# An expert layer on Trainium2: 128 slots in three split products, or 96 slots as three groups of 32 with unsplit weights in four column tiles

## The chip, the cores and the metric

One core of one Trainium2 chip. The metric is the device time of a run in microseconds; before the change the median of 3 runs is 1737.04 (1737.0 to 1737.24). Differences under 0.2% of that are not told from none.

## The reference

Two layers of a decoder trunk over 256 tokens of width 1024, all in float32: a mixer sub-layer with three token mixers, a cross-attention into a memory of 256 rows, and a channel sub-layer, which is a dense SwiGLU in layer 0 and eight experts in layer 1. The change touches only the experts:

```
def swiglu(h, w_gate, w_up, w_down):
    return (silu(h @ w_gate) * (h @ w_up)) @ w_down       # 1024 -> 2816 -> 1024

def moe_swiglu(h, w_router, w_gate, w_up, w_down):
    top_val, top_idx = lax.top_k(h @ w_router, 2)          # of 8 experts
    top_w = softmax(top_val)
    for e in range(8):
        out = out + comb[..., e:e+1] * swiglu(h, w_gate[e], w_up[e], w_down[e])
```

Each expert's three matrices are 34.6 MB, all eight 276.8 MB. For the given inputs the reference's own routing sends 74, 67, 63, 59, 76, 59, 64 and 50 of the 512 choices to the eight experts.

## The kernel before, in words

Each engine runs its own instruction list; semaphores order them. The list of the expert stage (layer 1) is built by `one_pass(p)` on every engine, which goes over the experts n = 0 to 7. A pass gives each expert 128 slots for tokens. A second pass stands in the program behind a branch (`moe_passes`, L588), and runs when an expert has more than 128 tokens.

The rows. The router's logits and counts give each token its slot. Expert 0's rows are gathered by a product with a 0/1 matrix (`gather`, L3328). Meanwhile GpSimd writes all rows of h, ordered by expert, to HBM with four indirect DMAs (L978), and later loads an expert's 128 rows as `h_e` (L983); TensorE transposes them (`turn_rows`, L3343) into `fx_e`, k on the partitions, slots on the free axis. The results of experts 0 to 6 are stored to `y_rows_d` in HBM (L986, L988), fetched per token by indirect DMA (L994) and added on VectorE. Expert 7's result is scattered by a product (`scatter`, L3350), added to x by VectorE (`add_scattered`, L2478 to L2484), and the last norm and the store of the output follow.

The products. float32 operands are split in a high and a low part of type fp32r, and a product is three matmuls (`split_product`, L3226): hi·hi, hi·lo, lo·hi. The stationary operand is a 128 x 128 block (128 of K, 128 slots), the moving one 128 x 512 of the weights. An expert is worked in chunks of 512 of its 2816 hidden columns, five full and one of 256: gate and up products (`input_group`, L3389), tanh on ScalarE (L1603), gating and multiplication by up on VectorE (`gated` L2514, `times_up` L2524), four transposes of the result (`flip`, L3370, counted under L3375), their split (L1595, L2508), and the down product (`output_groups`, L3400) into two PSUM banks. A chunk's flip stands inside the next chunk's gate product, and its down product after that chunk's up product.

The weights. SyncE's queue loads them in pieces of 128 partitions x 4096 floats (2 MB) into a ring of four buffers (L806 down, L815 gate and up, L823 the short chunk). A gate or up piece has runs of 512 columns (2 KB) in HBM, a down piece runs of 1024 (4 KB). A piece goes through `piece_hi` on ScalarE (L1089, copy to fp32r) and `piece_lo` on VectorE (L1696, subtraction) in two halves of 2048 columns, into four split buffers. SyncE may reuse a ring buffer when VectorE has split it, ScalarE a split buffer when TensorE has used it. The first four pieces are issued while the cross-attention of layer 1 still runs.

Elsewhere in the kernel unsplit float32 products occur. One form stands in the trace as two matmul records and two weight loads. Two of them are used below: full-array products of 128 x 256 (L2755), and the output of the state-space mixer, four column tiles of 32 each with its own moving operand:

```
for c in range(2):
    for i, r_ in enumerate(S5_ROWS):                       # r_ = 32 partitions of the bank
        last = mm(y_bank[r_, HS:SEQ], cT[:, c, q, r_], h(i, c), start=c == 0, stop=c == 1)
```

Of the kernel before, what the change touches and what calls it, by code (L numbers as in the profile page):

```python
# [7 lines left out]
def hybrid_trunk(nc: bass.Bass, x_d, mem_d, positions_d, norm_mix_d, w_in_d, a_re_d, a_im_d, log_dt_d,  # L8
# [40 lines left out]
    NPIECE, PIECE = 4, 4096  # L49
    NBUF, HGRP = 4, 2048  # L50
    assert D_FF == NFULL * FW + FC
# [61 lines left out]
    with ctx:  # L113
# [55 lines left out]
        gain_out = ring[:, NPIECE * PIECE:NPIECE * PIECE + D]  # L169
# [104 lines left out]
        def flat(v):  # L274
# [39 lines left out]
        rf.take(2 * KD * P + 2 * FC // P * SEQ)  # L314
        r_log = rf.take(NT, NE)
# [13 lines left out]
        gather_m = rf.take(NT, P)  # L329
        weight_m = rf.take(NT, P)  # L330
        scatter_m = rf.take(NT * P)
        y_e = rf.take(D)
# [4 lines left out]
        row_buf = [ring[:, NPIECE * PIECE + D:NPIECE * PIECE + 2 * D], h_e]  # L337
# [7 lines left out]
        y_rows_d = nc.dram_tensor("y_rows_d", ((NE - 1) * P + 1, D), F32, kind="Internal").ap()  # L345
# [13 lines left out]
        fx_e = [over("fx_e0", [P, 2, KD, P], phase_at + 4 * op_at),  # L359
                over("fx_e1", [P, 2, KD, P], qk_at + 4 * (6 * NT * W + 4 * D))]  # L360
        f_actT_e = over("f_actT_e", [P, 2, FW // P, P], phase_at + 4 * (op_at + 2 * KD * P))
        mf_th, mf_a, mf_act = (phase[:, i * FW:(i + 1) * FW] for i in range(3))
        split_e = [over("split_e0", [P, 2, HGRP], qk_at), over("split_e1", [P, 2, HGRP], qk_at + 8 * HGRP),
                   over("split_e2", [P, 2, HGRP], phase_at + 4 * end_at), over("split_e3", [P, 2, HGRP], hT_at)]
        assert 4 * HGRP <= 6 * NT * W + 2 * D and end_at + 2 * HGRP <= PH
        HI, LO = 0, 1

# [71 lines left out]
        B = [ctx.enter_context(nc.psum_tensor(f"bank{i}", [P, 512], F32)) for i in range(8)]  # L439
# [6 lines left out]
        piece_full = [slot_full[0], slot_full[1], sem("piece_full2"), slot_full[2]]  # L446
        split_hi, split_lo, split_used = sem("split_hi"), sem("split_lo"), sem("split_used")
        fx_hi, fx_ready, actT_hi = sem("fx_hi"), sem("fx_ready"), sem("actT_hi")
        ab_in, bc_nat_in = sem("ab_in"), sem("bc_nat_in")
        consts = sem("consts")  # L450
# [137 lines left out]
        def moe_passes(eng, one_pass, final=None):  # L588
            more = one_pass(0)
            if final is not None:  # L590
                with eng.If(more < 1):
                    final(0)
            with eng.If(more > 0):
                one_pass(1)
                if final is not None:
                    final(1)

        def last_piece(e, i):
            return (i % 2, i // 2) if e == NE - 1 else (i // 2, i % 2)
# [3 lines left out]


        def piece_base(l, s):
            return 0 if s == 2 else slot_after_unit(l, NUNIT - NSLOT + min(s, 2))

        group_at, piece_at, piece_end, piece_sum = {}, {}, [], []

        def count_piece(kind, n, c):  # L610
            half = c == NFULL
            s = len(piece_end) % NPIECE
            piece_at[kind, n, c] = len(piece_end)
            for i in range(1 if half and kind == "d" else 2):
                group_at[kind, n, c, i] = len(group_at)
            piece_end.append(len(group_at))
            piece_sum.append((piece_sum[-NPIECE] if len(piece_sum) >= NPIECE else 0)
                             + (32 if half and kind == "g" else 16))

        for p_ in range(2):  # L620
            for n_ in range(p_ * NE, (p_ + 1) * NE):
                for c_ in range(NFULL + 1):
                    count_piece("g", n_, c_)
                    if c_ < NFULL:
                        count_piece("u", n_, c_)
                    if c_ > 0:
                        count_piece("d", n_, c_ - 1)
                    elif n_ > p_ * NE:
                        count_piece("d", n_ - 1, NFULL)
            count_piece("d", (p_ + 1) * NE - 1, NFULL)  # L630

        def chunk_at(n, c):
            return n * (NFULL + 1) + c

        def chunk_before(n, c):
            return (n, c - 1) if c > 0 else (n - 1, NFULL)
# [9 lines left out]
        def scattered(n):  # L646
            return n >= NE - 1

# [3 lines left out]
        def closes(n, c):  # L652
            return n % NE == NE - 1 and c == NFULL

        def y_copies(n):
            return n + 1 if n < NE - 1 else NE - 1 + 2 * (n - (NE - 1) + 1)

        def act_buf(n, c):
            return fx_e[(n + 1) % 2] if closes(n, c) else f_actT_e
# [3 lines left out]

        def down_groups(c):
            return 2 if c < NFULL else 1

        def bank_turn(n, c, up):
            return n * (2 * NFULL + 1) + 2 * c + up

        def gate_bank(n, c):  # L670
            return bank_turn(n, c, 0) % 3

        def up_bank(n, c):
            return bank_turn(n, c, 1 if c < NFULL else 0) % 3
# [17 lines left out]
        def _(sp):  # L692
# [94 lines left out]
            def expert_pieces(l):  # L787
# [21 lines left out]
                def one_pass(p):  # L809
                    for e in range(NE):  # L810
                        n = p * NE + e
                        for c in range(NFULL):
# [4 lines left out]
                            if c > 0:  # L817
                                load_down(e, n, c - 1)
                            elif e > 0:
                                load_down(e - 1, n - 1, NFULL)  # L820
# [2667 lines left out]
```

## Time and profile before

| what | value |
|---|---|
| median of 3 runs | 1737.04 us |
| span of the profiled execution | 1733.9 us, 3.1 us under the median of the runs |
| PE / PEld busy | 1691.8 us (98%) / 1377.0 us (79%) |
| DVE / ACT / POOL busy | 1391.5 us (80%) / 1058.7 us (61%) / 158.5 us (9%) |
| HBM read | 422.93 MB, 250 GB/s over the span |
| granted TensorE clock, mean | 0.997 |

The execution's own time is known as its span, from the first to the last instruction. PE is TensorE's matmuls, PEld its weight loads, DVE VectorE, ACT ScalarE, POOL GpSimd, SP SyncE. Matmuls are pipelined and their ends are modelled, so that their recorded durations overlap: the pace is read from the distance between starts, not from a duration. A group's first row says how to read its view.

### The profile page before, as it was taken

The numbers are of one execution on the slowest core, as the hardware profiler recorded it, in microseconds if no ns is written. First come the engines' busy times: TensorE is split into PE (matmuls) and PEld (weight loads), VectorE is DVE, ScalarE is ACT, GpSimd is POOL, SyncE is SP. The second block draws the span as 40 slices with busy tenths as digits, with TensorE's granted clock in tenths as the row PEclk, the third lists the DMA queues.
The fourth block names the chain that finished last, engine by engine and source line by source line (L and its number), as shares of the span: only waits on it lengthen the run. The fifth ranks groups of instructions, "written<-read, shape, count | busy, mean of one in ns | idle before, by whom it ended". The sixth has DMA issues, their size and how long they took to land. (4 is left out here: it accounts for less than half of the span.)

```text
span 1733.9 us, 23684 instructions
## 1 busy us (share of the span) xinstructions
PE 1691.8 (98%) x9485; PEld 1377.0 (79%) x9485; DVE 1391.5 (80%) x1770; ACT 1058.7 (61%) x1228; POOL 158.5 (9%) x218
## 2 busy tenths in 40 slices
PE   8999999999999999999999999999999999999997
PEld 5778877788888888887778788888888888888885
DVE  5799677765555599967775899989998989899997
ACT  4335665555444533566556677777777777687765
POOL 7430002000000343000200100000000000000010
PEclk9999999999999999999999999999999999999999
DMA  9444543256551644444135699999999999999994
GB/s 269 146 146 164 177 146 135 98 194 217 195 192 50 212 147 146 162 178 146 50 110 206 243 391 380 396 368 395 373 395 370 393 388 378 390 376 390 356 397 167
DMA packets 220196, 434.93 MB, mean 251 GB/s; under 512 B 19180, under 2 KB 63864, under 8 KB 220088
## 3 DMA queue, kind: packets, MB, share of 16 engines
q1 hardware_dynamic: 213704, 419.45, 67.1%
q0 software_dynamic: 3520, 11.76, 1.8%
q10 hardware_dynamic: 2864, 2.23, 0.4%
q8 instruction: 73, 1.20, 0.3%
q14 instruction: 35, 0.29, 0.0%
HBM read 422.93 MB, written 10.49 MB: 250 GB/s over the span
## 5 line engine op out<-in xcount | busy, mean ns | idle before, releaser
L1696 DVE TENSOR_TENSOR split_e<-ring,split_e 128x2048 fp32r<-128x2048 f32 x264 | 598.4, 2287 | 40.2 <-ACT split_e L1089 39.9
L1089 ACT ACTIVATE split_e<-ring 128x2048 fp32r<-128x2048 f32 x264 | 503.3, 1919 | 149.5 <-PE bank L3230 130.9
L3228 PE MATMUL bank<-split_e,fx_e 128*128 128x512 f32 x708 | 280.3, 396 | 1.2 <-DVE split_e L1696 0.6
L3230 PE MATMUL bank<-split_e,fx_e 128*128 128x512 f32 x708 | 276.3, 390 | 0.0
L3229 PE MATMUL bank<-split_e,fx_e 128*128 128x512 f32 x708 | 275.8, 390 | 0.0
L3228 PEld LDWEIGHTS bank<-split_e,fx_e 128*128 128x128 f32 x708 | 133.0, 188 | 28.2 <-issue 0.8
L3230 PEld LDWEIGHTS bank<-split_e,fx_e 128*128 128x128 f32 x708 | 132.9, 188 | 28.3
L3229 PEld LDWEIGHTS bank<-split_e,fx_e 128*128 128x128 f32 x708 | 133.1, 188 | 26.3
L3228 PE MATMUL bank<-split_e,f_actT_e 128*128 128x512 f32 x348 | 136.1, 391 | 0.0
L3230 PE MATMUL bank<-split_e,f_actT_e 128*128 128x512 f32 x348 | 135.5, 389 | 0.0
L3229 PE MATMUL bank<-split_e,f_actT_e 128*128 128x512 f32 x348 | 135.4, 389 | 0.0
L1078 ACT ACTIVATE ring_r<-ring 128x1024 fp32r<-128x1024 f32 x71 | 73.9, 1057 | 53.5 <-PE bank L2781 47.1
L1690 DVE TENSOR_TENSOR ring_r<-ring,ring_r 128x1024 fp32r<-128x1024 f32 x71 | 84.7, 1219 | 22.6 <-ACT ring_r L1078 22.5
L2755 PE MATMUL bank<-hT,ring 128*128 128x256 f32 x384 | 85.0, 381 | 0.0
L2755 PEld LDWEIGHTS bank<-hT,ring 128*128 128x128 f32 x384 | 72.3, 190 | 10.6 <-issue 0.4
L3230 PEld LDWEIGHTS bank<-split_e,f_actT_e 128*128 128x128 f32 x348 | 65.3, 188 | 13.6
L3229 PEld LDWEIGHTS bank<-split_e,f_actT_e 128*128 128x128 f32 x348 | 65.4, 188 | 13.3
L3228 PEld LDWEIGHTS bank<-split_e,f_actT_e 128*128 128x128 f32 x348 | 65.3, 188 | 13.3
L3228 PE MATMUL bank<-split_mix,fx 128*128 128x512 f32 x168 | 66.4, 396 | 0.0
L3230 PE MATMUL bank<-split_mix,fx 128*128 128x512 f32 x168 | 65.5, 390 | 0.0
L3229 PE MATMUL bank<-split_mix,fx 128*128 128x512 f32 x168 | 65.4, 389 | 0.0
L1683 DVE TENSOR_TENSOR split_mix<-ring,split_mix 128x1024 fp32r<-128x1024 f32 x44 | 51.9, 1219 | 2.3 <-ACT split_mix L1057 1.6
(647 smaller groups left out, 3277.9 us busy)
## 6 DMA issues: line engine op xcount, KB each, us to landing
ring<-in_moe_w_gate SPq DMA_DIRECT2D x40, 2048.0 KB, 13.5
ring<-in_moe_w_up SPq DMA_DIRECT2D x40, 2048.0 KB, 13.4
ring<-in_moe_w_down SPq DMA_DIRECT2D x40, 2048.0 KB, 13.4
ring<-in_w_in SPq DMA_DIRECT2D x27, 2048.0 KB, 7.9
ring<-in_ffn_w_gate SPq DMA_DIRECT2D x11, 1024.0 KB, 5.4
ring<-in_ffn_w_up SPq DMA_DIRECT2D x11, 1024.0 KB, 8.0
ring<-in_ffn_w_down SPq DMA_DIRECT2D x11, 1024.0 KB, 8.7
ring<-in_ssm_w_glu SPq DMA_DIRECT2D x8, 1024.0 KB, 6.3
```

The source lines that it names most:

```text
L1078: nc.scalar.activation(unit_hi(l, m), unit_raw(j, i), ACT.Copy).then_inc(split_hi, 1)
L1089: nc.scalar.activation(split_e[j % NBUF][:, HI, :], ring[:, s * PIECE + i * HGRP:s * PIECE + (i + 1) * HGRP], ACT.Copy).then_inc(split_hi, 1)
L1683: V.tensor_tensor(split[buf][:, LO, :], raw_group(s, i), split[buf][:, HI, :].bitcast(F32), ALU.subtract).then_inc(split_lo, 1)
L1690: V.tensor_tensor(unit_lo(j, i), unit_raw(j, i), unit_hi(l, m).bitcast(F32), ALU.subtract).then_inc(split_lo, 1)
L1696: V.tensor_tensor(split_e[j % NBUF][:, LO, :], ring[:, s * PIECE + i * HGRP:s * PIECE + (i + 1) * HGRP], split_e[j % NBUF][:, HI, :].bitca ...
L2755: last = mm(B[t][:, (m % 2) * SEQ:(m % 2 + 1) * SEQ], w[:, k, m * P:(m + 1) * P], hT[:, k, :], start=k == 0, stop=k == KD - 1)
L3228: mm(bank, a[HI], w[HI], start=first, stop=False)
L3229: mm(bank, a[HI], w[LO], start=False, stop=False)
L3230: return mm(bank, a[LO], w[HI], start=False, stop=last_one)
```

## The change

The split of the expert weights goes, with `piece_hi`, `piece_lo`, `tail_hi`, `tail_lo`, `gathered_lo` and the fp32r buffers. Slots per expert become 96, as three groups of 32, with up to three passes behind the branch. Weights are used as they arrive, in unsplit float32 products of 128 x 32 stationary and 256 (in the last chunk 192) moving columns, four at a time in four column tiles that write to four quadrants of 32 PSUM partitions:

```
+        CAP, TG, GS = 96, 3, 32
+        CW = (1024, 1024, 768)
-        NPIECE, PIECE = 4, 4096
-        NBUF, HGRP = 4, 2048
+        NPIECE, PIECE, RING_PIECES = 7, 4096, 4

+                    def gate_or_up(kind, n, c):
...
+                        for i in range(2):
...
+                            cols = arrived_piece(kind, n, c, i)[:, 0:4 * CW[c]].rearrange("p (k f) -> p k f", f=CW[c])
+                            for k in range(4):
+                                kk = 4 * i + k
+                                for g in range(TG):
+                                    for j, r_ in enumerate(QUADS):
+                                        last = mm(out[r_, g, 0:w], fx_e[n % 2][:, kk, g * GS:(g + 1) * GS],
+                                                  cols[:, k, j * w:(j + 1) * w], start=..., stop=...)
+                            last.then_inc(split_used, 1)

+                    def down(n, c):
...
+                        for i in range(2):
+                            w = arrived_piece("d", n, c, i).rearrange("p (k n) -> p k n", n=D)
+                            for k in range(4 * i, min(4 * i + 4, last_k + 1)):
+                                for g in range(TG):
+                                    for j, r_ in enumerate(QUADS):
+                                        last = mm(y_out_bank[r_, g, :], acts(v, c, g, k), w[:, k % 4, j * CQ:(j + 1) * CQ],
+                                                  start=..., stop=...)

+                            for c in range(NC):
+                                gate_or_up("g", n, c)
+                                gate_or_up("u", n, c)
+                                if c == 1:
+                                    if closes(n):
+                                        turn_weights(n)
+                                    else:
+                                        turn_rows(n + 1)
+                                if chunk_before(n, c) is not None:
+                                    down(*chunk_before(n, c))
+                                flip(n, c)
+                            if closes(n):
+                                down(n, NC - 1)
+                                scatter(n)
```

A chunk is now 1024, 1024 or 768 hidden columns. Its gate and up results lie side by side in one of two sets of three banks (group by group, column quarter j in partition quadrant j), so tanh, gating and multiplication each run once over 128 x 3 x 256. The flip makes two transposes per group; in the last chunk one transpose and two products with a part of the identity, since a quarter is 192 wide:

```
+                    def flip(n, c):
...
+                        for g in range(TG):
+                            last = tr(to[:, g, 0:P], mf_act[:, g, 0:P], ident[:, :])
+                            if c < NC - 1:
+                                last = tr(to[:, g, P:2 * P], mf_act[:, g, P:2 * P], ident[:, :])
+                            else:
+                                for b in range(2):
+                                    last = mm(to[b * 64:(b + 1) * 64, g, P:192].rearrange(...), mf_act[:, g, P:192],
+                                              ident[:, :].rearrange(...)[:, b], start=True, stop=True)
```

A weight piece is still 128 x 4096 floats (3072 in the last chunk's gate and up), now four k tiles of 1024 columns, so its runs in HBM are 4 KB (3 KB). There are seven buffers, four in the ring and three over the space of q, k and the gates. A buffer is free when TensorE has used it:

```
+                free_after = [multiplied(l, U_OUT + 1), multiplied(l, U_WQ), multiplied(l, U_WQ), multiplied(l, U_WQ),
+                              (xs_o, XH * (l + 1)), multiplied(l, U_WO), (rows_in, 16 * ROWS_LAID)]
...
+                    if j >= NPIECE:
+                        sp.wait_ge(split_used, USED + j - NPIECE + 1)
+                    else:
+                        sp.wait_ge(*free_after[j])
```

ScalarE copies the gathered or turned rows and the flipped activations out of PSUM as they are. Expert results are stored to HBM in four DMAs instead of one. The last expert's result is scattered by products of K = 32 in four row tiles, and added to x in two additions of 1024 columns instead of four of 512.

## Rows read from the trace of the kernel before

**Rows 1.** Window sums: stretch, length, busy us (records) of each engine, PEclk, DMA share, GB/s.
```profile
960.00:974.00 14.00, 11.15 (x75) 10.81 (x73) 10.95 (x41) 6.77 (x13) 0.00 (x0) 0.76 0.79 299
974.00:1721.50 747.50, 746.64 (x3402) 617.86 (x3403) 682.29 (x437) 553.83 (x388) 21.99 (x22) 1.00 1.00 372
```

**Rows 2.** Records of one line (row turns): duration min/median/max, first and last start.
```profile
L3347 PE MATMUL bank<-ident,phase x56: 270/272/273, 1046.9 to 1607.6; 128*128 128x128 f32 x56
```

**Rows 3.** Waits from 1100 to 1600: us in total, times, longest.
```profile
ACT split_e L1089 <- PE bank L3230: 101.4, 142, 1.1
...
ACT split_e L1089 <- DMA ring<-in_moe_w_up: 0.9, 1, 0.9
```

**Rows 4.** Timeline of TensorE: start us, us, instruction; x4 is four merged.
```profile
1130.20 0.39 PE L3228 MATMUL bank<-split_e,fx_e 128*128 128x512 f32 x1
...
1130.88 0.39 PE L3228 MATMUL bank<-split_e,fx_e 128*128 128x512 f32 x1
...
1239.62 0.40 PE L3230 MATMUL bank<-split_e,f_actT_e 128*128 128x512 f32 x1
1239.85 0.60 PE L3375 MATMUL bank<-ident,phase 128*128 128x128 f32 x4
...
1240.53 0.39 PE L3229 MATMUL bank<-split_e,fx_e 128*128 128x512 f32 x1
```

**Rows 5.** Page, part 5: instruction groups, busy us, mean ns, idle before.
```profile
L1696 DVE TENSOR_TENSOR split_e<-ring,split_e 128x2048 fp32r<-128x2048 f32 x264 | 598.4, 2287 | 40.2 <-ACT split_e L1089 39.9
...
L3228 PE MATMUL bank<-split_e,fx_e 128*128 128x512 f32 x708 | 280.3, 396 | 1.2 <-DVE split_e L1696 0.6
...
L3228 PE MATMUL bank<-split_e,f_actT_e 128*128 128x512 f32 x348 | 136.1, 391 | 0.0
```

**Rows 6.** DMA: stretches of 4 KB packets and of 2 KB packets; issues with us to landing.
```profile
DMA packets 402, 1.65 MB, mean 412 GB/s; under 512 B 0, under 2 KB 0, under 8 KB 402
...
DMA packets 743, 1.54 MB, mean 384 GB/s; under 512 B 0, under 2 KB 0, under 8 KB 742
...
ring<-in_moe_w_gate SPq DMA_DIRECT2D x40, 2048.0 KB, 13.5
```

**Rows 7.** Timeline at the stage's start.
```profile
974.02 0.50 PE L3228 MATMUL bank<-split_e,fx_e 128*128 128x512 f32 x1 [0.36 <-DVE fx_e L2500]
...
993.04 0.60 POOL L983 DMA_DIRECT2D phase<-h_rows_d  x1 [7.70 <-DMA h_rows_d<-gates,row_at]
```

**Rows 8.** Timeline of TensorE around a tiled stretch; 128\*32 is rows and columns in use.
```profile
654.75 0.38 PE L2755 MATMUL bank<-hT,ring 128*128 128x256 f32 x1
655.06 0.42 PE L2826 MATMUL bank<-uT,phase 128*32 128x128 f32 x8
655.30 0.62 PE L2829 MATMUL bank<-phase 128*32 128x127 f32 x16
655.74 0.62 PE L2832 MATMUL bank<-phase 128*32 128x128 f32 x16
...
656.28 0.70 PE L2755 MATMUL bank<-hT,ring 128*128 128x256 f32 x2
...
656.82 4.26 PE L2755 MATMUL bank<-hT,ring 128*128 128x256 f32 x19
```

**Rows 9.** Instruction groups of ScalarE and VectorE, 1100 to 1600.
```profile
L1603 ACT ACTIVATE phase<-bank 128x512 f32<-128x512 f32 x27 | 15.7, 581 | 3.6 <-PE bank L3230 3.6
...
L2514 DVE SCALAR_TENSOR_TENSOR phase<-phase,bank 128x512 f32<-128x512 f32 x27 | 18.3, 680 | 0.0
```

**Rows 10.** Timeline at the end.
```profile
1721.53 3.94 PE L3358 MATMUL bank<-phase 128*128 128x512 f32 x8
...
1725.51 0.69 DVE L2484 TENSOR_TENSOR x<-x,bank 128x512 f32<-128x512 f32 x1 [0.27 <-PE bank L3358]
```

**Rows 11.** Weight loads of a tiled line: ns min/median/max.
```profile
L2829 PEld LDWEIGHTS bank<-phase x128: 110/110/110, 91.7 to 721.3; 128*32 128x32 f32 x128
```

**Rows 12.** Window sums: the 16 us with the most TensorE records.
```profile
276.97:292.97 16.00, 15.48 (x330) 13.30 (x332) 12.29 (x21) 5.81 (x11) 6.78 (x10) 1.00 0.44 142
```

More of the change, by code:

```diff
@@ L328, in hybrid_trunk @@
         over_i = sb("over_i", [P, 1], I32)
[L329 to L332, printed above, removed]
+        gather_m = rf.take(NT, CAP)
+        weight_m = rf.take(NT, TG, 4 * GS)
+        y_e = rf.take(TG, CQ)
+        re = Region(phase, rf_end)
+        fx_e = [re.take(KD, CAP) for _ in range(2)]
+        actT_e = [re.take(TG * CQ) for _ in range(2)]
+        scatter_m = re.take(NT, TG, P)
         xg = memT[:, :, :].rearrange("p k n -> p (k n)").rearrange("p (t n) -> p t n", t=NT)
@@ L608, in hybrid_trunk @@
[L608 to L630, printed above, removed]
         def chunk_at(n, c):
-            return n * (NFULL + 1) + c
+            return n * NC + c
@@ new lines, in count_piece @@
+        def count_piece(kind, n, c, i):
+            piece_at[kind, n, c, i] = len(piece_sum)
+            piece_sum.append((piece_sum[-NPIECE] if len(piece_sum) >= NPIECE else PIECE_BASE[len(piece_sum)])
+                             + (32 if kind == "d" and c == NC - 1 and i == 1 else 16))
+        for n_ in range(NALL):
+            for c_ in range(NC):
+                for kind_, nc_ in (("g", (n_, c_)), ("u", (n_, c_)), ("d", chunk_before(n_, c_))):
+                    if nc_ is not None:
+                        count_piece(kind_, *nc_, 0)
+                        count_piece(kind_, *nc_, 1)
+            if closes(n_):
+                count_piece("d", n_, NC - 1, 0)
+                count_piece("d", n_, NC - 1, 1)
@@ L3400, in output_groups, with scatter @@
-                    def output_groups(n, c, between=None):
-                        pe.wait_ge(actT_ready, base + chunk_at(n, c) + 1)
+                    def scatter(n):
+                        pe.wait_ge(sm_ready, scatter_turn(n) + 1)
+                        for t in range(NT):
+                            for g in range(TG):
+                                if g != 1:
+                                    pe.wait_ge(ye_ready, y_copies(n) - 1 + g // 2)
+                                for j, r_ in enumerate(QUADS):
+                                    last = mm(B[4 * t + j][:, 0:CQ], scatter_m[r_, t, g, :], y_e[r_, g, :],
+                                              start=g == 0, stop=g == TG - 1)
+                            last.then_inc(sc_ps, 1)
@@ new lines, in down @@
+                        last_k = 5 if ends else 7
+                        if ends and closes(n):
+                            w = [arrived_piece("d", n, c, i).rearrange("p (k n) -> p k n", n=D) for i in range(2)]
+                            for g in range(TG):
+                                for k in range(6):
+                                    for j, r_ in enumerate(QUADS):
+                                        last = mm(y_out_bank[r_, g, :], acts(v, c, g, k), w[k // 4][:, k % 4, j * CQ:(j + 1) * CQ],
+                                                  start=False, stop=k == last_k and g > 0)
+                                if g > 0:
+                                    last.then_inc(*((y_half, 1) if g == 1 else (split_used, 2)))
+                            return
```

571 lines of the change are left out of this document (225 added, 346 removed).

## The prediction

> **What bounds the kernel now.** I read the window sums first, to find the stretch that the change touches: the expert stage runs from 974.0 to 1721.5 us of the span and TensorE is busy through all of it [rows 1]. The last transpose of the last row turn starts 560.7 us after the first of the first, six experts earlier [rows 2]; less the seven transposes between (0.8), that is 93.3 us an expert, and 8 × 93.3 = 746.4 accounts for the stage. Next the waits: ScalarE waits for TensorE to hand back a split buffer (101.4 us in 500), for a weight DMA once (0.9 us) [rows 3]. So the others wait for TensorE. Last the pace inside: three products from 1130.20 to 1130.88 are 227 ns each, and from 1239.62 to 1240.53 two such steps, which else take 0.45 us, take 0.91 with four transposes between them, 0.11 each [rows 4]. An expert has 132 (k tile × 512 columns) blocks of three products: 396 × 0.227 = 89.9, and 22 + 8 transposes × 0.112 = 3.4; sum 93.3, the measured period, without any stall. The lines give the same counts: (708 + 348) / 8 = 132 [rows 5].
>
> DMA is the close second. The stage reads 372 GB/s, and a 2 MB piece lands 13.5 us after its issue although TensorE eats one every 24 × 0.227 = 5.4 us: two or three are always in flight [rows 1, 6]. With 4 KB runs alone the queue moves 412 GB/s, with 2 KB runs 384, at the same busy share of 102 to 103% [rows 6].
>
> **The change part by part.** *Splits out.* 264 VectorE subtractions and as many ScalarE copies go [rows 5]. They run beside TensorE and TensorE is not short of them: worth nothing on the path, except 0.5 us at the start, where TensorE waited until 974.02 for VectorE's half of the gathered rows [rows 7] and will now wait for the gather and ScalarE's copy only.
>
> *The products.* Now one unsplit fp32 product for K = 128, 32 slots, 256 columns, in each of four column tiles; three groups of 32 slots. I call four such products a round. The kernel before does the same in a small way: 128\*32 tiles with four different moving operands, 127 or 128 columns. A matmul of this kind stands in the trace as two passes. 16 passes take from 655.30 to 655.74, so four tiles' passes take 0.11 us together, what one tile's 128 columns would take alone: the tiles overlap fully [rows 8]. 256 columns are shown on the full array: (4.26 − 0.38) / 18 = 0.216 us a pass [rows 8]. I take 2 × 0.216 = 0.432 us for a round of 256 columns, and for the third chunk's 192 columns halfway between the two rows, 2 × 0.163 = 0.326. From below the cost is bounded by the 0.11 for 128 columns, doubled (0.44 a round, the same); from above by no overlap at all (4 × 0.432), which the 0.11 speaks against.
> An expert has for gate and up 2 × 8 k × 3 groups × 2 chunks = 96 rounds, 41.5 us, and 48 narrow ones, 15.6; for down 22 k × 3 = 66, 28.5. Sum 85.6 us against 89.9. The column count streamed is the same (96 slots unsplit cost what 128 slots in three products cost); the gain is that a pass costs 216 ns where the split product costs 227.
>
> *Transposes.* Flips 6 + 6 + 3, the row turn 8: 23 × 0.109 = 2.5 us; six 64-column products in the third flip, some 0.1 each (nearest the 0.11 rows), 0.5 in all.
>
> *Changes of tiling.* New: the array goes from 32-column tiles to full width and back four times an expert (three flips, the row turn), and inside the third flip five times between 128 and 64. From full to tiled, the first tiled pass starts 0.31 us after the last full one instead of 0.22, and the first round is 0.02 longer: 0.12. Back, 0.21: the last 16 passes start at 655.74 and would be through at 656.18, the full one starts at 656.28 and its successor 0.32 later, not 0.22 [rows 8]. 4 × 0.33 + 5 × 0.17 = 2.2 us. Bounds: zero, and twice that.
> An expert on TensorE: 85.6 + 2.5 + 0.5 + 2.2 = 90.8 us; eight, 726.4.
>
> *New exposed waits.* (a) The first chunk of the first expert has no down product between its up product and its flip. Tanh, gating and multiplication over 768 columns, one and a half times the 512-column rows (0.58, 0.68, 0.68) [rows 9], with 0.4 for hand-overs: 3.3 us once. Everywhere else 7.8 or 10.4 us of down product cover it. Behind the flip stand all of TensorE's later products. (b) The last flip is followed at once by its own down product: copy 0.87 + hand-overs 0.5 = 1.4 us.
> Stage: 726.4 + 3.3 + 1.4 = 731.1, against 747.5: −16.4.
>
> *DMA and its queue.* Seven buffers instead of four; SyncE issues in order, and piece 6 waits until the four indirect row stores have landed. They had at 993.04 [rows 7]; VectorE's part ahead of them loses a 2.3 us subtraction and the low halves, so about 989. The rest of the queue stands behind it. TensorE eats a piece in 12 rounds = 5.2 us from 973.5 on, with the 3.3 us stall after four, so it needs piece 6 at 1007 and piece 7 at 1012; issued at 989, they land by 996 and 1002. Hidden, with 10 us to spare; if the stores were 10 us later, each further us would be lost. Per expert 34.6 MB: 28.3 in 4 KB runs at 412 GB/s, 6.3 in 3 KB runs at the middle of the two rows, 398; 0.9 MB of rows and some fetch of the doubled instruction stream, 3.2 us: 87.7 us, under the 90.8. Storing y rows as four DMAs instead of one, and waits for them, have an expert's time to hide in.
>
> *Ends.* The scatter is 6 rounds (2.6 us) instead of 8 passes of 3.94, but its adds are 1024 wide and the last y copy is exposed; before, the last add starts 4.0 us after the scatter [rows 10]. +0.3.
>
> Sum: −0.5 − 16.4 + 0.3 = −16.6. The profiled span 1733.9 becomes 1717.3; the median of the runs lies 3.1 above that span, so **1720.5 us**.
>
> **A rule that speaks against it.** Row: in the tiled stretch every pass has its own weight load of 110 ns and the passes of a tile still follow each other every 0.11 us, so the loads are hidden [rows 8, 11]. The Trainium skill (TensorE: Matmul & The Clock Gate, "What overlaps and what doesn't") says that a weight load overlaps running matmuls only where its row group differs, which column tiles never offer; the trace disagrees for 128 columns. Its "Measured speedup" table gives three column tiles 2.38×, not 3×; an estimate by that share, 85.6 / 0.79, would be 108 us an expert and some 1899 us in all.
>
> **The rivals.**
> 1. *TensorE's instruction issue* (slower). A round is 16 instructions, 27 ns each at 256 columns and 20.4 at 192, for 15.6 us on end. For: the densest 16 us of the trace hold 330 + 332, that is 24.2 ns each [rows 12]. Against: TensorE also waits for others there, and the 32 matmuls and loads of 0.44 us came at 14 ns each [rows 8]. Were 24.2 a limit, each narrow round would take 387 instead of 326 ns: 48 × 0.061 × 8 = +23.4, **1744**. Above 23.1 ns it eats the whole gain (16.6 / 8 / 48 = 43 ns a round); at 30 ns the wide rounds suffer too, 1840.
> 2. *Weight loads not hidden at 256 columns* (slower): a round is 2 × (0.216 + 0.110), 0.546 narrow; 131.7 us an expert, +369: **2090**. This is the mechanism of the Trainium skill's rule above.
> 3. *DMA becomes the bound.* For: 87.7 against 90.8 is close, and after the change nothing shares the blame. All at 384 GB/s, the 272.6 MB that come after 989 are down at 1699, plus the last down product 7.8 and 2 for landing: 3 to 4 us late, **1724**; at the whole stage's 372, 1747. Against: 4 KB runs go faster [rows 6].
> 4. *Changes of tiling cost nothing*: TensorE needs 88.6, DMA 87.7: −17.6, **1703**.
> 5. *More than one pass*, if an expert had over 96 tokens: each pass repeats the stage. The reference's routing gives 74, 67, 63, 59, 76, 59, 64, 50, so no.
> The clock is a surcharge: it is granted at 0.76 on the mean in the router's gaps from 960 to 974 [rows 1]. If the 3.3 us stall brings it from 2.4 to 1.2 GHz for as long as there (0.24 × 14 × 2 = 7 us), 3.4 us are lost.
>
> **How the numbers follow.** Forecast 0.58, its own range 1711 to 1730. Rival 1: 0.15; 2: 0.04; 3: 0.12; 4: 0.10; 5: 0.01. Reaching to rivals 3, 4 and the near end of 1 leaves under 0.2 out: 1702 to 1743. A difference under 0.2% (3.5 us) can't be told from none. Faster: 0.58 + 0.10 + 0.09 = 0.77; same 0.07 (parts of 1 and 3); slower 0.16.
>
> **What would show it.** The distance between the first records of two row turns: 90.8 us (rival 4: 88.6; 1: 93.7 or more). Passes of a tile 216 ns apart, rounds in the third chunk 326; 387 there with 432 elsewhere is rival 1. A gap of 0.33 around each flip. One TensorE gap of 3.3 us ended by VectorE near 994, one of 1.4 before the last down product. TensorE waiting for DMA at most a few us in all; tens of us are rival 3. The forecast is wrong if TensorE's period is above 93 or below 89.

## The result, and the profile after

The changed kernel takes **1752.09 us** (median of 4 runs, 1750.18 to 1758.12); the kernel before took 1737.02 us on the same chip. The ratio is 1.0091, 95% interval 1.0074 to 1.0109: the change makes the kernel 0.9% slower. The forecast was 1720.5 us, range 1702 to 1743.

The page of the changed kernel (the first row of the span, the engines, and of part 3 the queue that brings instructions; columns as before):

```profile
span 1751.2 us, 43424 instructions
...
PE 1682.7 (96%) x19841; PEld 1251.6 (71%) x19841; DVE 752.3 (43%) x1396; ACT 548.2 (31%) x909; POOL 164.4 (9%) x239
...
q8 instruction: 153, 2.51, 0.6%
```

VectorE and ScalarE lost nearly half of their busy time, as the diff says, and it bought nothing. The window sum of the expert stage, to be set beside [rows 1]:

```profile
975.00:1743.00 768.00, 740.15 (x13746) 492.60 (x13738) 53.89 (x64) 54.03 (x80) 27.00 (x43) 0.99 0.98 360
```

The DMA engines are about as busy as before (0.98 against 1.00), but 372 GB/s have become 360. The records of the row turns, which answer to [rows 2]:

```profile
L3259 PE MATMUL banks<-ident,phase x56: 272/273/331, 1022.7 to 1582.9; 128*128 128x128 f32 x56
```

From the first transpose to the last (560.2 us) less the seven between (0.8) and over six experts, an expert takes 93.2 us. Forecast was 90.8, before it was 93.3. The six single distances rise: 91.2, 92.2, 93.3, 93.3, 93.7, 95.8. From the first transpose of the last row turn to the scatter's first product go another 153.8 us.

What TensorE waited for from 975 to 1740 (us in total, times, longest), to be set beside [rows 3]:

```profile
PE banks L3362 <- DMA ring<-in_moe_w_down: 6.1, 3, 4.3
PE banks L3312 <- issue: 5.9, 11, 1.1
PE banks L3312 <- DMA ring<-in_moe_w_up: 3.3, 4, 2.1
PE banks L3322 <- DVE phase L2478: 2.9, 1, 2.9
PE banks L3312 <- DMA past_ring<-in_moe_w_up: 2.3, 2, 2.1
PE banks L3362 <- issue: 1.4, 3, 0.6
PE banks L3352 <- ACT phase L1600: 0.7, 1, 0.7
PE banks L3312 <- DMA past_ring<-in_moe_w_gate: 0.7, 2, 0.5
```

Two things are new: waits for weights (12.4 us here), and "issue", gaps with no releaser in the profile (7.3 us). The 2.9 is the first flip, as forecast, and the 0.7 for ScalarE is the last one. Last, window sums within one expert:

```profile
1100.00:1153.00 53.00, 52.12 (x1028) 35.48 (x1024) 3.42 (x4) 3.15 (x5) 0.56 (x1) 1.00 1.02 400
1154.00:1164.00 10.00, 10.00 (x174) 6.11 (x175) 0.00 (x0) 0.65 (x1) 0.00 (x0) 1.00 1.03 229
1165.00:1240.00 75.00, 74.59 (x1438) 51.42 (x1434) 5.33 (x6) 5.56 (x8) 2.75 (x5) 1.00 1.03 404
```

For ten microseconds DMA moves 229 GB/s while the 16 engines show as fully busy. In the records of the packets, one of 4 KB takes about 300 ns there and 164 ns elsewhere. Such a stretch comes once an expert, in the place in the queue where the last chunk's down pieces stand. That is where the search began.

The end of the chain of waits (start us, us, what) shows what the shortage costs late, when the seven buffers' lead is used up:

```profile
1690.20 27.69 DMA ring<-in_moe_w_down
...
1717.93 7.74 PE banks L3362 x96
...
1728.00 7.98 PE banks L3352 x144
1735.98 1.56 PE banks L3281 x24
```

The first line is a down piece on its way for 27.69 us. TensorE waits 4.3 us for it and then runs at a granted clock of 0.51 (1.2 GHz) from 1715.9 to 1722.8: the x96 are 12 rounds, which took 7.7 us and not the 5.2 they need at 2.4 GHz.

### The profile page after: what moved, and what is told of

Read it like the earlier page. It is cut to its first block, busy times and chain, and to the rows that moved or that the text cites. A ratio compares the mean times of both kernels' runs of the same rounds, so it can differ in the third digit from the quotient of the medians.

```text
span 1751.2 us, 43424 instructions
## 1 busy us (share of the span) xinstructions
PE 1682.7 (96%) x19841; PEld 1251.6 (71%) x19841; DVE 752.3 (43%) x1396; ACT 548.2 (31%) x909; POOL 164.4 (9%) x239
## 4 chain that ended last, share of the span: by engine, by line
PE 81%; DMA 7%; DVE 6%; ACT 4%; issue 1%; POOL 1%; SPq 0%; DVEq 0%; ACTq 0%
PE banks L3312 23%; PE banks L3362 11%; DMA ring<-in_moe_w_up 5%; PE banks L2668 5%; PE banks L3141 3%; PE banks L3143 3%; PE banks L3142 3%; PE banks L2693 3%; PE banks L2697 3%; PE banks L2694 3%; PE banks L2601 3%; PE banks L2605 3%; PE banks L2602 3%; DMA ring<-in_moe_w_down 2%; PE banks L2876 1%; PE banks L2577 1%
## 5 line engine op out<-in xcount | busy, mean ns | idle before, releaser
L3312 PE MATMUL banks<-ring,phase 128*32 128x256 f32 (+1 forms) x5184 | 269.4, 363 | 6.9 <-DMA ring<-in_moe_w_up 3.3
L3312 PEld LDWEIGHTS banks<-ring,phase 128*32 128x32 f32 x5184 | 172.8, 110 | 95.8 <-issue 8.5
L3312 PE MATMUL banks<-past_ring,phase 128*32 128x256 f32 (+1 forms) x4032 | 210.9, 363 | 5.5 <-issue 2.5
L3312 PEld LDWEIGHTS banks<-past_ring,phase 128*32 128x32 f32 x4032 | 135.0, 111 | 74.0 <-issue 8.4
L3362 PE MATMUL banks<-ring,phase 128*32 128x256 f32 x2496 | 144.8, 384 | 6.7 <-DMA ring<-in_moe_w_down 6.1
L3362 PEld LDWEIGHTS banks<-ring,phase 128*32 128x32 f32 x2496 | 96.8, 111 | 49.3 <-issue 7.6
L3362 PE MATMUL banks<-past_ring,phase 128*32 128x256 f32 x1584 | 91.2, 379 | 0.8 <-issue 0.8
L2668 PE MATMUL banks<-hT,ring 128*128 128x256 f32 x384 | 85.0, 381 | 0.0
L2668 PEld LDWEIGHTS banks<-hT,ring 128*128 128x128 f32 x384 | 72.3, 190 | 10.6 <-issue 0.4
L3362 PEld LDWEIGHTS banks<-past_ring,phase 128*32 128x32 f32 x1584 | 59.8, 110 | 27.8 <-issue 2.5
L3141 PE MATMUL banks<-split_mix,fx 128*128 128x512 f32 x168 | 66.5, 396 | 0.0
L3143 PE MATMUL banks<-split_mix,fx 128*128 128x512 f32 x168 | 65.6, 390 | 0.0
L3142 PE MATMUL banks<-split_mix,fx 128*128 128x512 f32 x168 | 65.4, 389 | 0.0
L2693 PE MATMUL banks<-ring_r,merged_hi 128*128 128x512 f32 x128 | 50.9, 398 | 2.7 <-DVE ring_r L1665 2.1
```

What stands on the lines that cost most here:

```text
L2668: last = mm(B[t][:, (m % 2) * SEQ:(m % 2 + 1) * SEQ], w[:, k, m * P:(m + 1) * P], hT[:, k, :], start=k == 0, stop=k == KD - 1)
L2693: mm(bank[:, :], h_lo[:, k, at], hi, start=k == 0, stop=False)
L3141: mm(bank, a[HI], w[HI], start=first, stop=False)
L3142: mm(bank, a[HI], w[LO], start=False, stop=False)
L3143: return mm(bank, a[LO], w[HI], start=False, stop=last_one)
L3312: last = mm(out[r_, g, 0:w], fx_e[n % 2][:, kk, g * GS:(g + 1) * GS], cols[:, k, j * w:(j + 1) * w], start=kk == 0 and g in opens, stop=kk ...
```

## The experiments

Where an expert's time is given below, it comes from the row turns as above, (last start minus first, less 0.8) / 6. The kernel before ran at 1736.9 to 1738.1 us on the chips used.

**1. The last chunk's down pieces as plain loads.** Either piece, or both, is taken in natural row order (the products then meet the wrong rows; their number and form stay). Both:

```
-                 rows.rearrange("(j r) n -> r j n", r=192)[0:P]).then_inc(piece_full[s], 16)
+                 down[e][:, 16:20, :]).then_inc(piece_full[s], 16)
...
-        for b in range(2):
-            sp.dma_start(to[b * 64:(b + 1) * 64, 0:2 * D]..., ends[b, P:192]).then_inc(piece_full[s], 16)
+        sp.dma_start(to[:, 0:2 * D]..., down[e][:, 20:22, :]).then_inc(piece_full[s], 16)
```

> The last chunk's two down pieces are loaded as plain rows, 128 partitions each, as all other down pieces are; the rows land in other places than the products take them for, so the output is not the reference's. In the changed kernel 4 KB packets take twice as long (some 300 ns instead of 164) for 10 to 15 us once an expert, at about 225 GB/s, and the place in the queue fits these two pieces. Theory A (transfers into 64 partitions run at half rate) and theory B (rows taken 192 apart) both expect the slow stretch gone: an expert every 90.8 to 91.5 us on TensorE, no wait of 4.7 us before the last down product, 1720 to 1732 us. Rival C (the queue is slow for another reason, the shape of the pieces has no part in it): slow stretch stays, 1748 to 1756.

Measured 1728.82 us, ratio 0.9955 (0.9939 to 0.9972), 91.6 us an expert.

> Only the first of the two pieces (2 MB, 128 partitions) is loaded as plain rows instead of rows 192 apart; the output is not the reference's. Theory A: slow stretch stays nearly as it is, 1745 to 1755. Theory B: two thirds of it go, 1728 to 1738. Rival C: 1748 to 1756.

Measured 1747.06 us, 1.0049 (1.0032 to 1.0066), 93.1 us an expert; the slow stretches stay.

> Only the second piece (1 MB) is loaded by one transfer into 128 partitions instead of two into 64 each; the output is not the reference's. Theory A: the slow stretch goes, 1720 to 1735. Theory B: two thirds of it stay, 1742 to 1750. Rival C: 1748 to 1756.

Measured 1727.36 us, 0.9943 (0.9926 to 0.9960), 91.4 us an expert; the slow stretches are gone:

```profile
1100.00:1240.00 140.00, 136.88 (x2633) 90.41 (x2629) 8.74 (x10) 9.35 (x14) 3.31 (x6) 1.00 1.00 385
```

So 24.7 us hang on the second piece alone, 1 MB an expert, which the changed kernel brings in two transfers of 64 partitions. Rows 192 apart (the first piece) matter little: 5.0 us while the halves are there, and nothing once they are gone (1728.8 against 1727.4).

**2. Less traffic, halves kept.** From the second expert on, gate and up pieces load three of four k tiles.

```
+    nk = 4 if n == 0 else 3
+    sp.dma_start(to[:, 0:nk * CW[c]]..., w[n % NE][:, 4 * i:4 * i + nk, ...]).then_inc(piece_full[s], 16)
```

> From expert 1 on the gate and up pieces load three quarters of their bytes (the last k tile is left as it was, the output is not the reference's); TensorE does all its work. The slow stretch stays, but DMA has 5.6 MB an expert less to move, 14 us at 400 GB/s. If DMA is what bounds the changed kernel, TensorE's own period of 90.5 to 91.5 us shows and the time is 1720 to 1728. If TensorE itself is slower than forecast (issue, or weight loads), the period stays at 92 to 95 and the time above 1740.

Measured 1729.40 us, 0.9945 (0.9924 to 0.9966), 91.2 us an expert, with the slow stretches still there: the period is as expected, the time 1.4 us above the expected range. With bandwidth to spare they cost almost nothing: they hurt because DMA has too little slack to make them good.

**3. The same row order made whole.** This kernel computes everything. The two pieces are loaded plainly. VectorE writes the odd quadrants of the third chunk rotated, so that the turned pieces match natural 128-row tiles:

```
+    for j in range(4):
+        r_ = slice(j * GS, (j + 1) * GS)
+        for a, b, z in ((0, 0, w),) if j % 2 == 0 else ((64, 0, P), (0, P, 64)):
+            last = V.tensor_tensor(mf_act[r_, :, b:b + z], mf_a[r_, :, a:a + z],
+                                   up_cols(v)[r_, :, a:a + z], ALU.mult)
+    last.then_inc(act_ready, 1)
...
+    k = (0, 4, 1, 2, 5, 3)[k]
     at = k * GS if k < 4 else P + (k - 4) * GS
```

> The whole reference computed, with the last chunk's down weights fetched in their natural row order, by two transfers over all 128 partitions. VectorE writes the odd quadrants of the last chunk rotated (columns 64 to 191 first, then 0 to 63) in six small multiplications instead of one, and the down products take the turned pieces in the order 0, 4, 1, 2, 5, 3. Theory A (transfers into 64 adjacent partitions run at half rate; nothing else is wrong with the change): 1727 to 1729 us, as with the plain second piece alone (1727.4), expert period 90.8 to 92, no stretch with 4 KB packets of 300 ns. The five more VectorE instructions lie behind 7.8 us of down product and cost nothing. Rival (the gain of the two plain-load kernels came from wrong rows being cheap, not from the transfer): nothing in it changes the transfers' form, so it has no number under 1745 to give. If the VectorE chain is exposed at the third flip: 8 x 1 us more, 1736.

Measured 1730.69 us, 0.9962 (0.9948 to 0.9976), 91.5 us an expert, 1.7 us above the expected range. TensorE's waits in its stage to 1690:

```profile
PE banks L3316 <- issue: 3.9, 5, 1.4
PE banks L3326 <- DVE phase L2475: 2.9, 1, 2.9
PE banks L3367 <- issue: 1.0, 2, 0.7
```

No wait for weights, and the one wait for VectorE is the first flip's: the five more instructions at the third flip cost nothing. With four buffers (NPIECE = 4):

> The natural-order kernel with four piece buffers instead of seven. Theory: TensorE eats a piece in 5.2 us, a piece lands 13.5 us after its issue at the full rate, three are ahead of the one in use, so four buffers do: 1727 to 1731 us. Rival (the queue has to be deep because TensorE's instruction fetches and the pieces disturb each other, or because a landing takes 17 us as with seven buffers): TensorE waits for DMA some 2 us an expert, 1743 us or more.

Measured 1728.39 us, 0.9954 (0.9941 to 0.9967), 91.1 us an expert. Seven buffers bring nothing once the transfers are whole. Together with the kernel of even and odd partitions below (1728.12 us), from which it can't be told, this is the fastest here that computes the whole reference.

**4. TensorE's own time.** As the natural-order kernel, but most pieces load one k tile of four.

```
+    nk = 4 if n == 0 else 1
```

> The natural-order kernel; from the second expert on, a gate or up piece loads one k tile of four, and the down pieces of the first two chunks too, so output is not the reference's; every product and wait stays. It asks for TensorE's own time and what the instruction fetches do without the weight traffic. Theory D (TensorE's gaps of 0.5 to 2.4 us that end 1.2 to 1.5 us behind an instruction fetch are fetches held up by weight packets in the same 16 DMA engines): gaps gone, expert periods 90.2 to 90.8 us, 1721 us. Rival E (the fetch chain is too slow for 20.3 ns per instruction whatever the traffic): the gaps stay, 6 to 9 us in all, 1727 us. Rival F (TensorE also waits for weights unseen): under 1718.

Measured 1721.58 us, 0.9906 (0.9891 to 0.9921). All six distances are 90.3 us. Its row turns, and all that TensorE waited for from 975 to 1700:

```profile
L3264 PE MATMUL banks<-ident,phase x56: 272/273/328, 1027.5 to 1570.1; 128*128 128x128 f32 x56
```

```profile
PE banks L3327 <- DVE phase L2476: 2.9, 1, 2.9
PE banks L3317 <- issue: 0.3, 1, 0.3
```

The gaps put down to "issue" all but vanish with the weight traffic, though TensorE issues at the same pace. In the fuller kernels (the changed one, natural order, adjacent halves) each ends 1.2 to 1.7 us after the end of a 16 KB packet of the instruction queue, but for one of 3.3 at the stage's start. I read them as instruction fetches that wait behind weights. The fetch packets themselves take 1.0 us (median) with the full traffic of natural order and with a quarter of it, so the wait must lie ahead of them, where no record shows it. Between this kernel and the natural-order one are 9.1 us; the gaps in the latter are 5.2 in all. A gap is counted only from the end of the last product's recorded duration: from start to start the six stalls between the first and the last row turn are 5.8 us, of the 7.2 by which the six periods differ. The rest of the 9.1 is not assigned. With quarter loads but the changed kernel's halves:

> The changed kernel's last down pieces with their halves of 64 partitions, but from the second expert on all other gate, up and down pieces load a quarter (the output is not the reference's). DMA has idle time then (60% with plain pieces). Theory H (the half rate costs because DMA has no time to spare): nothing is lost, periods 90.3 us as with the quarter loads and plain pieces, 1721.6 us. Rival I (slow packets hold up instruction fetches whatever else is queued): 0.5 to 4 us of TensorE gaps an expert, each ended by a fetch, 1726 to 1750 us.

```profile
L3260 PE MATMUL banks<-ident,phase x56: 272/273/329, 1025.2 to 1567.7; 128*128 128x128 f32 x56
```

Measured 1720.20 us, 0.9904 (0.9888 to 0.9921), again 90.3 us: theory H. In the packets' records some 190 an expert more are slow here than with quarter loads and no halves; in the full queue it is 600 to 700.

**5. DMA's own time.** The changed kernel, and the natural-order one, with `for k in (0, 3):` in place of `for k in range(4):` in the gate and up products.

> The changed kernel with all its transfers; of the gate and up products only the first and last k tile of each piece are taken (72 rounds of 144 an expert left out, 28.5 us), so TensorE alone would need 90.3 - 28.5 = 61.8 us an expert and the transfers set the pace. It measures what the prediction had as 87.7 us an expert. Theory: the 1 MB in half partitions costs 2.3 us more than at the full rate; period 91 to 93.5 us, about 1740 us. Rival (TensorE, or the fetch of its instructions, sets the changed kernel's 93.3 us): below 90 us here.

> The same with the natural-order kernel's transfers (all over 128 partitions). Theory: 2 to 3 us an expert under the kernel with half partitions; by the forecast's rates 87.7 us, by the 390 GB/s that the natural-order kernel moved 91.3 us. I expect 89 us: at 91 the natural-order kernel's 91.3 is DMA's and not the instruction fetches'; at 88 it is the fetches'. In all 1705 to 1728 us.

Window sums from 1020 to 1650, of the changed transfers and of the whole ones, each with its row turns ahead of it:

```profile
L3259 PE MATMUL banks<-ident,phase x56: 272/273/330, 1002.7 to 1568.1; 128*128 128x128 f32 x56
```

```profile
1020.00:1650.00 630.00, 471.25 (x7572) 281.75 (x7572) 36.92 (x46) 40.90 (x59) 18.24 (x33) 0.91 1.02 379
```

```profile
L3263 PE MATMUL banks<-ident,phase x56: 272/273/330, 1003.8 to 1532.5; 128*128 128x128 f32 x56
```

```profile
1020.00:1650.00 630.00, 493.45 (x8083) 302.16 (x8078) 58.06 (x85) 43.36 (x62) 22.92 (x37) 0.93 1.02 406
```

DMA alone needs 94.1 us an expert with the halves (379 GB/s) and 88.0 without (406 GB/s). The medians are 1746.99 us (8 runs, 1739.71 to 1751.12; the profile is of the shortest) and 1691.31 us (2 runs). Their distance over eight experts is 7.0 us an expert, against 6.1 between the profiled executions. In the profile the slow packets account for it: about 690 an expert, each 0.14 us longer, over 16 engines, are 6.0 us. I had expected 2.3: that is what 1 MB costs at half rate if only its own packets are slow. The natural-order period is 1 us under what I expected, and its total is 14 us under the expected range of 1705 to 1728.

**6. Another piece in halves.** In the natural-order kernel the first gate piece of each later expert (2 MB) goes by two transfers, first into adjacent halves, then into even and odd partitions.

```
+    for b in range(2):
+        sp.dma_start(to[b * 64:(b + 1) * 64, 0:4 * CW[c]]...,            # then: to[b:P:2, ...]
+                     w[n % NE][b * 64:(b + 1) * 64, 0:4, 0:CW[0]]).then_inc(piece_full[s], 16)
```

> The natural-order kernel; from the second expert on, the first gate piece of each expert (2 MB, 16 KB per partition, 4 KB runs) is fetched by two transfers, into partitions 0 to 63 and 64 to 127, instead of one. Theory A: twice the bytes of the changed kernel's split piece at half rate, so DMA loses twice its 4.5 to 5.8 us, 9 to 11 us an expert, of which 3 are hidden under TensorE: 7 experts x 6 to 8 us, 1770 to 1785 us. Rival G (the last chunk's rows 192 apart and the half partitions have to come together, or one more transfer is what costs): within 2 us of the natural-order kernel.

Measured 1759.62 us, 1.0123 (1.0108 to 1.0139), 96.0 us an expert. Two window sums, within the stretch and behind it, and TensorE's waits from 975 to 1730:

```profile
1136.00:1144.00 8.00, 7.55 (x179) 5.34 (x167) 0.00 (x0) 0.00 (x0) 0.00 (x0) 1.00 1.02 215
1146.00:1166.00 20.00, 18.07 (x316) 15.15 (x320) 3.90 (x7) 0.92 (x2) 0.00 (x0) 0.91 1.02 407
```

```profile
PE banks L3321 <- issue: 25.0, 12, 4.1
PE banks L3331 <- DVE phase L2480: 3.0, 1, 3.0
```

The place is as expected, the size less (4.5 us an expert more, not 6 to 8), and the form was a surprise: TensorE waits for no weight; what comes late is instructions. Some 700 packets an expert are slow, hardly more than with the changed kernel's 1 MB, so the loss does not grow in step with the bytes that go in halves.

> As the kernel with the first gate piece of each later expert in two transfers of 64 partitions (1759.6 us), but one transfer goes to the even and one to the odd partitions instead of 0 to 63 and 64 to 127. Same bytes, runs, number of transfers and packets. Theory A (what slows the packets is that all 16 engines write to neighbouring partitions at once): packets stay at 164 ns, 1730 to 1732 us as with one transfer (1730.7). Rival G (64 partitions a transfer, or the second transfer, is what costs, wherever they lie): 1757 to 1762 us again with 300 ns packets.

Measured 1728.12 us, 0.9950 (0.9934 to 0.9967), 91.4 us an expert, with no slow stretch (some 200 slow packets an expert are scattered over it, as in the natural-order kernel). Neither the second transfer nor 64 partitions in one is what costs; where they lie is.

**7. Split by run.** The changed kernel, its row order kept, the second piece split the other way: each transfer takes one 4 KB run of all 128 partitions.

```
-        ends = rows.rearrange("(m b r) n -> b r m n", b=2, r=192)
+        ends = rows.rearrange("(m b r) n -> m b r n", b=2, r=192)
+        for m in range(2):
+            sp.dma_start(to[:, m * D:(m + 1) * D], ends[m, :, P:192]).then_inc(piece_full[s], 16)
```

> The changed kernel whole, its row order kept; the last chunk's second down piece still comes in two transfers of 0.5 MB, but one brings the first 4 KB run of all 128 partitions and the other the second, instead of both runs of partitions 0 to 63 and both of 64 to 127. Theory A (transfers into 64 neighbouring partitions run slow): 1727 to 1731 us, no stretch of 300 ns packets, periods 90.5 to 92. Rival J (small transfers, or rows from three places, are what costs, and the earlier plain loads removed them as well): 1745 us or more.

> The same with four piece buffers instead of seven. Theory: with four, three pieces are ahead, as many as the 13 to 15 us of a landing need, and fewer packets are queued before an instruction fetch: 1726 to 1730 us, TensorE's gaps behind fetches 5 us in all instead of 6 to 8. Rival (seven buffers bring something): 2 us or more slower than with seven.

Measured 1877.66 us, 1.0807 (1.0793 to 1.0822), and 1895.06 us, 1.0906 (1.0886 to 1.0925). I was wrong by 150 us. Of the first, DMA from 1064 to 1072 in 40 slices, and the wait for the piece from 1020 to 1800:

```profile
DMA  7776944424120110101101101101111011011019
GB/s 287 307 287 266 348 164 164 143 82 143 61 82 41 41 82 41 41 41 82 41 41 61 61 41 41 82 41 41 61 61 41 41 82 41 41 41 82 41 41 225
```

```profile
PE banks L3361 <- DMA ring<-in_moe_w_down: 54.6, 4, 19.4
PE banks L3361 <- DMA past_ring<-in_moe_w_down: 51.8, 3, 17.9
```

At 41 to 61 GB/s two of 16 engines are at work (410 / 16 = 26 each): 256 packets of 0.164 us on two engines are 21 us, near the longest wait of 19.4. The transfers' source has an outermost dimension of 2, the half-row blocks. The Trainium skill (DMA: Bandwidth & Descriptors, "Why a DMA increments its semaphore by 16 and not by 1") says that a transfer is spread over the largest number of engines, 16 at most, that divides the outermost dimension of both its sides. By that rule, 2; the trace agrees. So this was no test of the halves; and as the queue runs dry in it, no test of the buffers. It shows one thing that I had not looked for. The weight transfers behind the dry stretch all cover 128 partitions, and still:

```profile
1076.00:1090.00 14.00, 14.00 (x268) 8.42 (x263) 1.91 (x2) 0.81 (x1) 0.00 (x0) 1.00 1.03 263
```

With all engines busy the queue moves 263 GB/s there for 14 us, and most of its packets take over 200 ns. So packets of whole transfers can be slow behind a transfer that covers no half.

**8. Which 64 partitions.** The kernel of DMA's own time with whole transfers (88.0 us), but the first gate piece of each later expert loads only 64 partitions, in one transfer: half the piece is left out.

```
+    sp.dma_start(to[32:96, 0:4 * CW[c]]..., w[n % NE][32:96, 0:4, 0:CW[0]]).then_inc(piece_full[s], 16)   # or 0:64
```

> The natural-order kernel with half its gate and up products, so that DMA alone sets the pace (88.0 us an expert with every piece whole). From the second expert on, the first gate piece of each expert loads only partitions 32 to 95: 1 MB instead of 2, in one transfer of 64 neighbouring partitions. At the full rate the MB left out is worth 2.6 us: 85.4 us an expert. Theory K (what counts is whether a transfer has partitions on both sides of 64, as 32 to 95 has): packets of 164 ns, 85.4 us an expert, about 1673 us in all. The Trainium skill (SBUF — State Buffer, Door 1: The DMA port swizzle) states such a map of partitions to 16 ports. Theory A as first put (64 neighbouring partitions are slow wherever they lie): slow as with partitions 0 to 63, 88 to 91.5 us an expert, 1691 to 1715 us.

> The same with partitions 0 to 63 instead of 32 to 95: same bytes, runs, number of transfers and rows in a transfer. Both theories: packets near 300 ns in a stretch of some 5 to 10 us an expert; 85.4 + 2.6 to 6.1 = 88 to 91.5 us an expert, 1691 to 1715 us. If it equals the kernel with partitions 32 to 95, neither holds for a single transfer, and it takes the pair of halves to make them slow.

Row turns and the window from 1036 to 1042, within the piece's time, first for partitions 32 to 95, then for 0 to 63:

```profile
L3267 PE MATMUL banks<-ident,phase x56: 272/273/330, 1004.2 to 1519.3; 128*128 128x128 f32 x56
```

```profile
1036.00:1042.00 6.00, 6.00 (x112) 4.36 (x108) 0.00 (x0) 0.00 (x0) 0.00 (x0) 0.96 1.02 408
```

```profile
L3267 PE MATMUL banks<-ident,phase x56: 272/273/476, 1002.2 to 1565.7; 128*128 128x128 f32 x56
```

```profile
1036.00:1042.00 6.00, 4.43 (x84) 2.61 (x80) 0.00 (x0) 0.00 (x0) 0.00 (x0) 1.00 1.03 207
```

1675.57 us (2 runs) and 85.7 us an expert against 1724.77 (8 runs, 1711.83 to 1732.35) and 93.8, above what either theory gave it. The same 1 MB, in the same number of rows and packets, costs 8.1 us more in partitions 0 to 63 than in 32 to 95. That is between the profiled executions, of which the second is the slowest of its eight; by the medians it is 7.0 (49.2 over seven experts). On which partitions are slow theory K holds, as far as 0 to 63 goes (64 to 127 were not loaded alone); "64 neighbouring partitions", as I first put theory A, is refuted. The Trainium skill (SBUF — State Buffer, "Door 1: The DMA port swizzle (why [64,N] ≈ [32,N])") has the map: the bit of a partition's number that is worth 64 picks one of two sets of 8 ports, so 0 to 63 reach 8 of 16, and it gives some 218 GB/s for them. The traces agree in rate (207 to 229 against 404 to 408 GB/s), and in that transfers into even or odd partitions and into 32 to 95 go at the full rate. The cost is larger than by the rule alone: an estimate for 1 MB at half rate is 1 / 0.207 − 1 / 0.408, times 1.05, 2.5 us.

## Why the prediction was wrong

**What held.** TensorE's side, nearly to the tenth: 90.8 us an expert forecast, 90.3 measured with most of the traffic out of the way. So four column tiles do overlap at 256 columns, weight loads stay hidden (rival 2 falls, and the estimate of 1899 us with it), tilings cost something when they change, if less than forecast (0.31 us from the last tiled pass to a flip's first transpose, where passes are 0.22 apart; rival 4 would need 88.6), and instruction issue as such is no limit (rival 1 falls: passes of a tile in the narrow rounds are 163 ns apart, as forecast). The x144 of the last down product, 18 rounds, took 7.98 us, forecast 7.8. The first flip's gap was 3.3 us from start to start, the last flip's 0.97 against 1.4. So the whole kernel takes 1721.6 us there; forecast 1720.5.

**The step that failed** is the sum under "DMA and its queue": "28.3 in 4 KB runs at 412 GB/s ... 87.7 us, under the 90.8". For whole transfers it is right: 88.0 measured. The changed kernel's are not all whole. The diff shows `to[b * 64:(b + 1) * 64, ...]` for the last chunk's second piece; I priced it by its run length, as [rows 6] do, and never asked which partitions a transfer covers. Of the kernel before no row shows such a transfer in the stage, so it needed a bound and had none. With the halves the term is 94.1 us in the profiled execution and nearer 95 by the medians, so it was 6 to 7 us too small. That makes DMA the bound: 1747.0 us with half of gate and up products left out, 5 us under the changed kernel. The forecast's own sign of being wrong, a period above 93, is there at 93.2. Rival 3 had this outcome, but from run lengths, at 0.12, and its upper price of 1747 came from the whole stage's rate and not from a cause.

**A second term was missing.** Fetch was counted as bytes, in DMA's sum, and for a stream that doubles. Over the whole kernel TensorE's stream does (9485 to 19841 products), but in the stage it is four times as dense (3402 records in [rows 1], 13746 now). A 16 KB packet of instructions comes every 6.8 us instead of 27, and with the engines full of weights some come late: they are most of the 9.1 us between 1721.6 and 1730.7. The Trainium skill (Runtime: NRT & Kernel Launch, "Instruction fetch mechanics") calls such fetches mostly hidden. The traces agree where DMA has idle time (0.3 us of gaps with quarter loads), and not in the full queue (5.2 us in natural order, 25.0 with adjacent halves).

**The sum as it is.** 1721.6 TensorE and ends; +9.1 the full weight traffic, mostly fetches held up; +21.4 the halves (1730.7 to 1752.1), which come as waits for weights (12.4 us of gaps, against none), as more late instructions (7.3 against 5.2) and as the low clock behind the longest wait. Within the changed kernel's stage, of its 762.3 us from first product to scatter against 731.1 forecast, 14.6 are lost over the six middle experts (559.4 against 6 × 90.8) and about as much (14.8) behind the last row turn, against the quarter-load kernel's 139.0 there. That fits seven buffers that first cover the shortage and then are empty; that they are why so much falls at the end was not tested by itself.

**What stays open.** Why 1 MB in halves slows 600 to 700 packets and not its own 256. The others are those of whole transfers queued near it; with DMA half idle some 190 more are slow. That whole transfers were also slow behind the two-engine ones of experiment 7 speaks for something that outlasts the transfer itself; what it is, was not tried. So the halves as the cause of the loss are shown, and the way from them to 6 or 7 us is not.

## What to carry to other kernels

Price each transfer by the partitions that it covers and by its outermost dimension, as well as by its run length: a small piece on one side of partition 64, or one whose outer dimension is 2, can cost a saturated queue several times its own share. The runs of such a kernel also spread more (11 and 21 us over eight here, against 1 us at most over two with whole transfers), so compare medians and not two profiles. Where DMA and TensorE are within a few per cent of each other, measure each alone (halve the other's work) before either is tuned. A denser instruction stream needs DMA time that is free when the fetch comes, and not just the bytes; look for "issue" gaps that vanish with the traffic.

## What the runs showed of the hardware beyond that

A half on one side of partition 64 brings the queue from 408 to 207 to 229 GB/s, and for longer than its own bytes: by the medians 7.0 us an expert for 1 MB, in two halves as in one (6.1 and 8.1 between the profiled executions, the shortest and the slowest of their eight). The 16 engines show a mean busy share of 1.02 to 1.03 meanwhile, so the share does not tell a slow port from a full queue; the GB/s beside it do. Even and odd partitions (407 GB/s), and partitions 32 to 95 (408), go at the full rate. A source of outermost dimension 2 runs at 41 to 61 GB/s, and whole transfers behind it at 263.
